# Regrouping one tile's TensorE work in the mixing stage: shared product with logits, turn inside the attention's projection

## The reference, cut to what matters

```python
x  = ln_affine(DN_ALPHA * x + gate1 * (concat(rms_norm(att), rms_norm(lru)) @ w_out), ln1_g, ln1_b)
u  = ln_plain(x) * (1 + scale2) + shift2
scores = sigmoid(u @ w_router)                     # 64 experts: the logits
# best 4 of 8 groups, best 6 experts of them, weights scaled to a sum of 2.5
g, up = split(u @ w_sh_in, 2)                      # the shared expert, 256 + 256 columns
shared = (silu(g) * up) @ w_sh_out
y = ln_affine(DN_ALPHA * x + gate2 * (routed + shared), ln2_g, ln2_b)
```

## Time and profile before

| | |
|---|---|
| median of 3 runs | 2910.28 us (2909.89 to 2911.74) |
| the profiled execution | 2911.56 us |
| its span, first to last instruction | 2909.7 us |
| mean granted TensorE clock | 0.978 of full speed |
| busy: TensorE, VectorE, ScalarE, GpSimd | 95%, 54%, 24%, 37% |
| mixing: first projection, experts' first product | 986.06 us, 1477.20 us |

### The profile page before, as it was taken

One profiled execution on the slowest core, in us unless ns is written; L12 is line 12 of the kernel. 1 busy time (PEld: TensorE's weight loads), 2 busy tenths in 40 slices (PEclk: granted clock), 3 DMA queues, 4 the chain that ended last, 5 costly groups with the idle time before them and its releaser, 6 DMA issues.

```text
span 2909.7 us, 31340 instructions
## 1 busy us (share of the span) xinstructions
PE 2750.7 (95%) x9145; PEld 1322.5 (45%) x9145; DVE 1584.6 (54%) x2551; ACT 692.2 (24%) x1204; POOL 1075.5 (37%) x1129
## 2 busy tenths in 40 slices
PE   6999999899999899899899999999999999999991
PEld 2345444455555454454444444444444444444440
DVE  3467356778877467787743333333333333344336
ACT  2354254366666211112100000000000000000004
POOL 2002000100000113233456665666665666565554
PEclk9999999999999999999999999999999999999996
DMA  8531010310000311221178798987888788899847
GB/s 336 192 114 55 17 34 8 129 42 12 12 12 8 142 44 66 87 80 59 59 247 252 202 322 246 294 257 188 271 232 251 184 247 247 258 304 292 237 94 253
DMA packets 188242, 464.37 MB, mean 160 GB/s; under 512 B 21500, under 2 KB 46270, under 8 KB 186750
## 3 DMA queue, kind: packets, MB, share of 16 engines
q1 hardware_dynamic: 137246, 311.89, 30.1%
q0 software_dynamic: 50912, 151.41, 21.3%
HBM read 359.28 MB, written 99.75 MB: 158 GB/s over the span
## 4 chain that ended last, share of the span: by engine, by line
PE 58%; DVE 5%; DMA 1%; issue 1%; POOL 1%; ACT 0%; DVEq 0%; POOLq 0%
PE mx_pH L1270 30%; PE mx_pU L1287 15%; PE mx_pA L1877 3%; PE mx_pH L1901 3%; PE mx_pL L1877 2%; PE mx_pU L1924 2%; PE mx_pB L1257 1%; DVE ring L1401 1%; DVE mx_st L1713 1%; DMA s_acc<-mx_wso,ex_sidx 1%; PE mx_pB L1913 1%; PE mx_pA L1901 0%; PE mx_pU L1887 0%; POOL mx_sm L1584 0%; DMA kT<-in_w_out 0%
## 5 line engine op out<-in xcount | busy, mean ns | idle before, releaser
L1270 PE MATMUL mx_pH<-ring,mx_wsi 128*128 (+1 forms) x2080 | 937.1, 593 | 5.0 <-DVE mx_wsi L1184 3.0
L1104 POOL DMA_INDIRECT kT<-s_u,ex_gidx x516 | 570.9, 1106 | 158.9 <-issue 153.2
L1270 PEld LDWEIGHTS mx_pH<-ring,mx_wsi 128*128 128x128 f32 x2080 | 385.5, 190 | 442.2 <-issue 442.2
L1287 PE MATMUL mx_pU<-qT,mx_hT 128*128 x1040 | 467.6, 592 | 1.5 <-DVE mx_wso L1211 1.5
L1184 DVE STREAM_TRANSPOSE mx_wsi<-kT 128x1024 f32<-128x1024 f32 x130 | 161.6, 1243 | 323.9 <-DMA kT<-s_u,ex_gidx 323.5
L1287 PEld LDWEIGHTS mx_pU<-qT,mx_hT 128*128 128x128 f32 x1040 | 197.5, 190 | 250.0 <-issue 250.0
L1128 POOL DMA_INDIRECT s_acc<-mx_wso,ex_sidx x130 | 212.2, 1633 | 188.6 <-DVE mx_wso L1211 126.5
L1211 DVE SCALAR_TENSOR_TENSOR mx_wso<-mx_pU,mx_wsi 128x1024 f32<-128x1024 f32 x130 | 166.9, 1284 | 194.9 <-PE mx_pU L1287 190.1
L1158 ACT ACTIVATE mx_hT<-mx_pB 128x256 f32<-128x256 f32 x130 | 49.9, 384 | 866.8 <-PE mx_pB L1257 866.8
L1188 DVE TENSOR_TENSOR mx_h<-mx_silu,mx_pH 128x256 f32<-128x256 f32 x130 | 54.6, 420 | 320.8 <-ACT mx_silu L1148 320.4
L638 PE MATMUL fr_pF<-fr_uT,fr_wf 128*128 128x512 f32 x512 | 224.9, 595 | 1.3 <-ACT fr_uT L332 1.0
(11 more groups left out here) (312 smaller groups left out, 3162.7 us busy)
## 6 DMA issues: line engine op xcount, KB each, us to landing
ring<-in_w_exp_in SPq DMA_DIRECT2D x64, 2048.0 KB, 12.8
qT<-in_w_exp_out SPq DMA_DIRECT2D x64, 1024.0 KB, 15.7
fr_wq<-in_w_ada SPq DMA_DIRECT2D x32, 512.0 KB, 4.8
kT<-s_u,ex_gidx POOLq DMA_INDIRECT x520
fr_wf<-in_w_in SPq DMA_DIRECT2D x16, 512.0 KB, 5.6
s_u<-v SPq DMA_DIRECT2D x16, 512.0 KB, 2.7
ring<-s_acc SPq DMA_DIRECT2D x16, 512.0 KB, 12.9
y<-ring SPq DMA_DIRECT2D x16, 512.0 KB, 3.7
```

What stands on the lines that cost most here:

```text
L1104: nc.gpsimd.indirect_dma_start(xg[:, u, g, :], None, u2_q, bass.IndirectOffsetOnAxis(ap=gidx[:, u, g:g + 1].bitcast(U32), axis=0)).then_in ...
L1270: m = nc.tensor.matmul(pH[:], xT[:, u, k, :], wi[:, bass.ds(slot, 1), k, :].rearrange("p a f -> p (a f)"), start=(k == 0), stop=(k == KD - 1))
L1287: m = nc.tensor.matmul(pY[:, h, :], hT[:, c, :], wo[:, bass.ds(slot, 1), c, h * 512:(h + 1) * 512].rearrange("p a d -> p (a d)"), start=(c ...
```

## The change

The logits of a tile become part of its shared product. The router's weights move into the tile of the shared weights, as columns 0 to 63 of each contraction slice. Up to tile LATE, `shared_in` is now two products: 64 + 256 = 320 columns (logits and the silu half) into `pH`, and 256 columns (the up half) into `pB`, which has a semaphore `up_mm`; the separate logits are left only behind LATE.

TensorE's order in iteration i (1 to LATE) becomes: att(i) half 0; turn(i); att(i) half 1; shared_in(i); lru(i+1) half 0; gated(i); rank(i-1); lru(i+1) half 1; shared_out(i). The lru product of a tile stands one iteration earlier.

On VectorE `gate(i-1)` moves from ahead of `add_att(i)` into the second statistics of `norms(i)`, between the statistics and the aggregate; `add_shared(i-1)` moves from `norms(i)` into `router(i-1)`, ahead of the one-hot of the six experts. On ScalarE `scores` comes before `gated_rows` and reads `pH`. On SP the store of a tile's sum comes one iteration later, and the load of x stands directly behind it.

```diff
...
   sem = lambda n: ctx.enter_context(nc.semaphore("mx_" + n))
-  wr, wsi, wso = sb("mx_wr", [P, KD, N_EXP]), sb("mx_wsi", [P, KD, 2 * D_E]), sb("mx_wso", [P, NB, D_E // P, D])
+  wsi, wso = sb("mx_wsi", [P, KD, 2 * D_E + N_EXP]), sb("mx_wso", [P, NB, D_E // P, D])
   rb, ln, iota, tokf = sb("mx_rb", [P, N_EXP]), sb("mx_ln", [P, 2, D]), sb("mx_iota", [P, N_EXP]), sb("mx_tokf", [P, 1])
...
   R1, R2, V1, V2 = range(4)
-  LOG, RNK = 0, 64
+  UP, LOG, RNK = 0, D_E, D_E + N_EXP
+  FIRST = N_EXP + D_E
...
       load_x(1)
-      sp.dma_start(wsi[:], w_sh_in.rearrange("(k p) f -> p k f", p=P)).then_inc(w_in, 16)
+      sp.dma_start(wsi[:, :, N_EXP:], w_sh_in.rearrange("(k p) f -> p k f", p=P)).then_inc(w_in, 16)
       gate2 = lambda b: mod_d[b:b + 1, 5 * D:6 * D].partition_broadcast(P)
...
       sp.dma_start(g2[:], gate2(0)).then_inc(g2_in, 16)
-      for dst, src in ((wr[:], w_router), (rb[:], router_bias.partition_broadcast(P)), (iota[:], iota_d.partition_broadcast(P))):
+      for dst, src in ((wsi[:, :, 0:N_EXP], w_router), (rb[:], router_bias.partition_broadcast(P)), (iota[:], iota_d.partition_broadcast(P))):
           sp.dma_start(dst, src).then_inc(r_in, 16)
...
                   load_wo(c)
-          if 0 < i <= LATE:
-              store_z(i - 1)
+          if 2 <= i <= LATE + 1:
+              store_z(i - 2)
+          if i >= 2 and i + 1 < NT:
+              load_x(i + 1)
           sp.wait_ge(u2_ready, i + 1)
...
               load_wo(7)
-          if i and i + 2 < NT:
-              load_x(i + 2)
           if i == KT:
...
           act.wait_ge(ut_mm, i)
-          if i > 1:
-              act.wait_ge(log_mm, i - 1)
+          if 1 < i <= LATE + 1:
+              act.wait_ge(up_mm, i - 1)
+          elif i > 1:
+              act.wait_ge(log_mm, i - 1 - LATE)
           if LATE < i < NT:
...
       def silu(i):
           act.wait_ge(h_mm, i)
...
               act.wait_ge(h_ready, i - 1)
-          nc.scalar.activation(silu_of(i), bank_of(i)[:, 0:D_E], ACT.Silu).then_inc(silu_ready, 1)
+          nc.scalar.activation(silu_of(i), bank_of(i)[:, N_EXP:FIRST] if i <= LATE else bank_of(i)[:, 0:D_E], ACT.Silu).then_inc(silu_ready, 1)
...
       def scores(i, logits):
-          act.wait_ge(log_mm, i)
+          if i <= LATE:
+              act.wait_ge(h_mm, i)
+              logits = pH[:, 0:N_EXP]
+          else:
+              act.wait_ge(log_mm, i - LATE)
           if i > 2:
...
               silu(i)
-              gated_rows(i)
           scores(i, pB[:, LOG:LOG + N_EXP])
+          if i <= LATE:
+              gated_rows(i)
       silu(LATE + 1)
...
-      def stats(z, which, eps, var_col, done):
+      def stats(z, which, eps, var_col, done, amid=None):
           for c in range(2):
...
           passed(dve, apart)
+          if amid is not None:
+              gate(amid)
           step(nc.vector.bn_aggr(mv[:, which, :], st[:].rearrange("p a s -> p (a s)")))
...
           dve.wait_ge(x1_ready, i + 1)
-          stats(z, 1, EPS, V2, var2)
+          stats(z, 1, EPS, V2, var2, i - 1 if 0 < i <= LATE else None)
           if i >= 2:
...
           step(nc.vector.scalar_tensor_tensor(u, z, mv[:, 1, 0:1], mrow[:, i // KT, 1, :], ALU.subtract, ALU.mult))
-          if 0 < i <= LATE:
-              add_shared(i - 1)
           dve.wait_ge(rstd2, i + 1)
...
           dve.wait_ge(silu_ready, i + 1)
-          nc.vector.tensor_tensor(gated_of(i + 1), silu_of(i + 1), bank_of(i + 1)[:, D_E:2 * D_E], ALU.mult).then_inc(h_ready, 1)
+          up = bank_of(i + 1)[:, D_E:2 * D_E]
+          if i < LATE:
+              dve.wait_ge(up_mm, i + 1)
+              up = pB[:, UP:UP + D_E]
+          nc.vector.tensor_tensor(gated_of(i + 1), silu_of(i + 1), up, ALU.mult).then_inc(h_ready, 1)
-      def router(i):
+      def router(i, amid=None):
           by_rank = lambda a, n: a.unsqueeze(1).to_broadcast([P, n, a.shape[1]])
...
           step(nc.vector.tensor_copy(gf[:, 1, :], gi[:, 1, :]))
+          if amid is not None:
+              add_shared(amid)
           step(nc.vector.tensor_tensor(oh[:], by_rank(iota[:], TOP_K), by_item(gf[:, 1, 0:TOP_K], N_EXP), ALU.is_equal))
...
                   fold(c)
-          if 0 < i <= LATE:
-              gate(i - 1)
           add_att(i)
...
           if i:
-              router(i - 1)
+              router(i - 1, i - 1 if i <= LATE else None)
       ranks(NT - 2)
...
+      def lru_half(i, h):
+          if i and h == 0:
+              pe.wait_ge(l_added, i)
+          if i == KT and h == 0:
+              pe.wait_ge(wo_folded, GQ)
+          m = project(pL, 1, lruT, i, h)
+          if h:
+              m.then_inc(pl_mm, 1)
       def project(out, which, src, i, h):
...
               pe.wait_ge(r_in, 48)
+          if i <= LATE:
+              for k in range(KD):
+                  m = nc.tensor.matmul(pH[:, 0:FIRST], uT(i, k), wsi[:, k, 0:FIRST], start=(k == 0), stop=(k == KD - 1))
+              m.then_inc(h_mm, 1)
+              if i > 1:
+                  pe.wait_ge(h_ready, i - 1)
+              if i > 2:
+                  pe.wait_ge(slots_ready, i - 2)
+              for k in range(KD):
+                  m = nc.tensor.matmul(pB[:, UP:UP + D_E], uT(i, k), wsi[:, k, FIRST:], start=(k == 0), stop=(k == KD - 1))
+              m.then_inc(up_mm, 1)
+              return
           for k in range(k0, k1):
-              m = nc.tensor.matmul(bank_of(i), uT(i, k), wsi[:, k, :], start=(k == 0), stop=(k == KD - 1))
+              m = nc.tensor.matmul(bank_of(i), uT(i, k), wsi[:, k, N_EXP:], start=(k == 0), stop=(k == KD - 1))
           if k1 == KD:
...
           pe.wait_ge(h_ready, i)
+          if i <= LATE:
+              pe.wait_ge(ez_ready, i)
           for c in range(FC):
...
           for k in range(KD):
-              m = nc.tensor.matmul(out, uT(i, k), wr[:, k, :], start=(k == 0), stop=(k == KD - 1))
+              m = nc.tensor.matmul(out, uT(i, k), wsi[:, k, 0:N_EXP], start=(k == 0), stop=(k == KD - 1))
           m.then_inc(log_mm, 1)
...
           pe.wait_ge(ez_ready, read)
+          pe.wait_ge(h_ready, min(read, LATE))
           if i > 1:
...
+      lru_half(0, 0)
+      lru_half(0, 1)
       for i in range(NT):
           if i:
-              pe.wait_ge(l_added, i)
-          if i == KT:
-              pe.wait_ge(wo_folded, GQ)
-          project(pL, 1, lruT, i, 0)
-          project(pL, 1, lruT, i, 1).then_inc(pl_mm, 1)
-          if i:
-              turn(i)
               pe.wait_ge(a_added, i)
...
           if i:
+              turn(i)
+          project(pA, 0, attT, i, 1).then_inc(pa_mm, 1)
+          if i:
               pe.wait_ge(ut_copied, i)
...
               shared_in(i)
-          project(pA, 0, attT, i, 1).then_inc(pa_mm, 1)
-          if 0 < i <= LATE:
+              lru_half(i + 1, 0)
               gated(i)
-          if i:
-              if i > 1:
-                  pe.wait_ge(ez_ready, i - 1)
-              if i > 2:
-                  pe.wait_ge(slots_ready, i - 2)
-              logits(i, pB[:, LOG:LOG + N_EXP])
-          if 0 < i <= LATE:
+              if i >= 2:
+                  rank(i - 1, i)
+              lru_half(i + 1, 1)
               shared_out(i)
-          if i >= 2:
+          elif i:
+              if i == LATE + 1:
+                  pe.wait_ge(h_ready, LATE)
+              pe.wait_ge(ez_ready, i - 1)
+              pe.wait_ge(slots_ready, i - 2)
+              logits(i, pB[:, LOG:LOG + N_EXP])
+          if i > LATE:
               rank(i - 1, i)
+          if (i == 0 or i > LATE) and i + 1 < NT:
+              lru_half(i + 1, 0)
+              lru_half(i + 1, 1)
```

More of the change, by code:

```diff
@@ L1486, in mixing @@
             [sem("u2_stored0"), sem("u2_stored1")])
-        ut_mm, ut_copied, h_mm, silu_ready, h_ready, ht_mm, ht_copied = (sem("ut_mm"), sem("ut_copied"), sem("h_mm"), sem("silu_ready"), sem("h_ready"),
+        up_mm, ut_mm, ut_copied, h_mm, silu_ready, h_ready, ht_mm, ht_copied = (sem("up_mm"), sem("ut_mm"), sem("ut_copied"), sem("h_mm"), sem("silu_ready"), sem("h_ready"),
                                                                         sem("ht_mm"), sem("ht_copied"))
@@ L1655, in _ @@
                     silu(i)
+                scores(i, pB[:, LOG:LOG + N_EXP])
+                if i <= LATE:
                     gated_rows(i)
-                scores(i, pB[:, LOG:LOG + N_EXP])
             silu(LATE + 1)
@@ L1958, in _ @@
                     shared_in(i)
-                project(pA, 0, attT, i, 1).then_inc(pa_mm, 1)
-                if 0 < i <= LATE:
+                    lru_half(i + 1, 0)
                     gated(i)
-                if i:
-                    if i > 1:
-                        pe.wait_ge(ez_ready, i - 1)
-                    if i > 2:
-                        pe.wait_ge(slots_ready, i - 2)
+                    if i >= 2:
+                        rank(i - 1, i)
+                    lru_half(i + 1, 1)
+                    shared_out(i)
+                elif i:
```

(8 more changed lines are left out.)

## The result

The changed kernel takes **2893.76 us** (median of four runs, 2891.93 to 2896.62), the kernel before 2910.86 beside it: a ratio of 0.994, 95% interval 0.9926 to 0.9954, so 17.1 us less. 2893.3 was predicted. The profiled execution took 2891.93 with a span of 2889.4, against 2911.56 and 2909.7 before.

What follows compares the result with a forecast made beforehand. TensorE's list was taken to bound most mixing tiles, VectorE the stage's end. Tiles of 26.46 us, a warm start and the earlier refold less turn 8's wait gave 17.0 us: 2894.6 profiled, 2893.3 median, range 2888 to 2903.

Steps and rivals of the forecast that it cites:

- What bounds: Mixing stage, tiles 1 to 6 and 8 to 12: TensorE's list sets the end, 27.36 us a tile before.
- The merged passes: Shared product with logits: passes of 320 and 256 columns take 7.74 us instead of 8.60, 0.86 off each tile.
- The tile: TensorE's new order in an ordinary tile of the mixing stage sums to 26.46 us, with no added hand-off cost.
- VectorE's round: VectorE's work per tile ends at 24.8 us, leaving 1.7 us slack; shared sum 1.8 us ahead of the turn.
- Start: Stage start: att 1's first half fills TensorE's 4.23 us gap, so turn 1 comes warm at 1012.61.
- Refold: Weight refold after tile 7: att 8 starts 15.5 us earlier, but turn 8 waits 3 to 5 us for shared sum 7.
- the slow price: After turn 8's idle, TensorE was taken to run slow: 1.69 us for the turn, 4.6 for the att half.
- Covered edits: ScalarE, SP and GpSimd edits and the router's weights load stay hidden; the load may land up to 7 us later.
- The sum: VectorE adds att 13 at 1349.4 instead of 1366.44, a gain of 17.0 us carried to the stage's end.
- A: Rival: merged passes pay weight load beside columns and cost the same, giving 2901.9 us; chance 0.04.
- C: Rival: turns wait for the shared sum in every tile, slower than before, 2919.7 us at 4.2 late; chance 0.05.
- B: Rival: only the merge pays, the reordering gives back its start and refold gains, 2901.7 us; chance 0.05.

Runs made afterwards that it cites:

- Experiment 4: Changed kernel without the merged product: shared product of 512 columns again, the logits' 16 passes of 64 right behind it; 2903.52 us, ratio 0.9968 to the kernel before.
- experiment 7: The changed kernel itself, unaltered, measured again beside other kernels; 2893.53 us, ratio 0.9935 to the kernel before.
- Experiment 8: Changed kernel with shared sum 7 alone moved right behind the refold's last fold, out of the router; 2890.88 us, ratio 0.9926 to the kernel before.
- Experiment 5: Changed kernel with the turn ahead of the first half of the attention's projection instead of between its halves; 2921.68 us, ratio 1.0035 to the kernel before.
- experiment 1: Kernel before with the merged 320- and 256-column products, old order kept except ScalarE's exponential ahead of its rows copy; 2916.01 us, ratio 1.0013.
- experiment 2: Merged product in the old order, as in experiment 1, with the ranks' product moved between gated rows and shared output; ratio 1.0014 to the kernel before.
- experiment 3: Experiment 1's kernel with the first normalisation's last pass cut to 64 of 1024 columns in tiles 1 to 12; tile 27.21 us, median not compared.

## Why the prediction was right, point by point

- **What bounds.** Right: TensorE's list in tiles 1 to 6 and 8 to 12, busy throughout at 1.00 but for the 0.46 us of tile 2 below.
- **The merged passes.** 320 columns were priced at 0.269 us and cost 4.31/16 = 0.269; 256 at 0.216 and cost 3.45/16 = 0.216. The product took 7.76 for 7.74. Experiment 4, which differs in this alone, has a tile 0.89 longer where 0.86 was the term. The Trainium skill ("TensorE: Matmul & The Clock Gate", Part 3, section "The mechanism") says that a weight load overlaps matmuls in flight only where it goes to another row group; read as in the prediction, by which load and columns add up and nothing is saved, this does not hold for these passes: the window of the tile above has 15.15 us of weight loads (PEld) inside 26.50 us, and a pass costs 0.84 ns per column at 256, 320 and 512. The same section also lets a load into the background weight buffer go ahead of matmuls in flight; no run here shows which buffer these loads went to.
- **The tile.** 26.46 predicted, 26.47 measured; hand-offs between accumulation groups cost 0.01.
- **VectorE's round.** Counted from VectorE adding att: shared sum at 19.14 of the round predicted, 18.9 measured; its lead on the turn 1.8, as measured; slack ahead of att 1.7 predicted, 1.96 measured. The gate waited 0.34 us where I had 0.14 (it came at 7.83 instead of 7.77), since the up half's result follows its slot by a latency, without effect.
- **Start.** Turn 1 was put 26.55 us into the stage, warm, and came at 26.50, warm. Tile 2's second fold was to cost 0.4; the tile took 26.93, 0.46 more than the others.
- **Refold.** Att 8 was to start at 216.3 and started at 216.0; turn 8 at 224.7, measured 224.2; att 8 was to be added at 231.0, measured 230.5. Att 7 was added 0.4 us later than forecast (196.07 for 195.6), and att 8 started 0.7 sooner behind it than forecast; the two misses offset each other, which is luck. The choice of the slow price (1.69 and 4.6, in all 6.3) was right in sum, 1.28 and 4.75 by the starts, and 0.99 and 5.03 in experiment 7. Experiment 8 shows that this wait was a real cost of the change. It took back 3.1 to 3.9 us of stage where I had expected 4.
- **Covered edits.** The store and load of x, the list writes and the exponential ahead of the rows nowhere show as a wait of TensorE in tiles 2 to 6. The first shared product did not wait for the router's weights: it started at 1015.17, right behind its att half.
- **The sum.** Att 13 was to be added 17.0 us earlier; it came 17.56 earlier in the stage, and the stage ended 17.23 earlier.

**The rivals.** A is out by the passes themselves. C did not occur. Experiment 5 shows its wait costing somewhat more than I gave it: 22.2 us of stage without the 5.1 at the start, where C's sum gives 11 x 1.74 = 19.1. B said that only the merge pays. It was the opposite, and this is where my working was weakest: it took 8.6 us as the merge's own worth, whatever the order. Experiments 1 and 4 make the four corners (stage against before's):

| | passes of 512 and 64 | passes of 320 and 256 |
|---|---|---|
| old order | 0 | +3.8 |
| new order | -6.6 | -17.2 and -16.4 |

Without the slow first passes of that execution the -6.6 is -8.1, and the merge is worth 8.3 to 9.1 us in the new order, near ten tiles of 0.89. The forecast didn't need the missing corner, since it added up TensorE's list in the new order directly. But a reader of it would have built the merge by itself for 8.6 us and lost 3. What the new order does for the merge is to put the products behind both att halves, out of the way from att to u to turn to att, and to give lru halves as cover for gate and copy. That the loop sets the tile in the old order is shown by experiments 2 and 3 together. The +3.8 splits into 0.9 up to att 1, 1.1 from there to att 6, 1.9 to att 8 and 0.7 to att 13, less 0.8 behind it; experiment 2 has 1.1, 2.1 and 0.7 for the three stretches in the middle. Of the 1.9, the longer product is 0.9 and an att half that ran slower, behind 6.31 us of idle instead of 3.58, is 0.4 (5.55 by the starts for 5.11); why the att half also started 0.6 later is open.

Left open: whether the 1.75 us by which front and attention ended earlier is spread. Their instructions are the same, and the eight kernels' mixing stages started between 983.83 and 985.74, all earlier than before's 986.06, of which only one execution has a trace.

## What to carry to other kernels

Work that an engine does between two dependent steps is cover as well as cost: before taking it out, list what ran behind it (here a copy, and the write of u), and sum the loop over the other engines as well as the engine's own list. The gain is at most the distance to the second longest of these, and work that is moved can lengthen one of them, as the logits did here. When a reordering makes a consumer wait for work on a busy engine, give it its place for the tiles where that engine has more to do (a fold, a reload), not only for the ordinary one: the ordinary tile of experiment 5 was foreseen to 0.1 us, and its stage missed by 8 (19 us over the changed kernel's expected, 27.4 measured).

## What the runs showed of the hardware

A narrow fp32 pass is held up by something other than its columns, a pass of 256 is not: 64 columns cost 1.73/16 = 0.108 us apiece, 256 cost 0.216, 320 cost 0.269, 512 cost 6.87/16 = 0.429. Per column of the last three that is 0.84 ns each time. The eight transposes of a turn, of 128 columns each, take 0.87 us, 0.109 apiece: as much as 64 columns of a product.

Idles of TensorE and the granted clock behind them: 0.80, 1.55 and 2.22 us left the work behind fast (turns 0.93 and 0.90, an att half 3.51 by the starts), 3.18, 3.70, 4.23 and 4.52 left it slow (the att half behind the last 4.91 instead of 3.60), and so did the 3.58 of the earlier trace rows (5.27). The idle of 3.56 in the earlier trace rows left a fast turn. In the tiles behind the twelfth shorter ones went either way: experiments 1 and 2 both idle 2.43 us ahead of turn 14, which took 1.09 us at a granted clock of 1.00 in the one (1380.60 to 1382.00), 1.97 at 0.50 in the other (1382.54 to 1384.50); in after, the recurrence's product behind 2.14 us of idle had 0.73 (1369.92 to 1375.50). So the length of the idle alone does not decide.

With the router's weights landing in 256-byte pieces, the queue that issues stood still behind their load; TensorE did not wait longer for them. SyncE's timeline of after:

```profile
992.25 1.14 SPq L1532 DMA_DIRECT2D mx_wsi<-in_w_router  x1
993.43 9.40 SPq L1532 DMA_DIRECT2D mx_rb<-in_router_bias  x1
1002.87 0.43 SPq L1532 DMA_DIRECT2D mx_iota<-in_iota  x1
```

The next load behind it took 9.40 us to issue (0.60 before), and 9.47 to 10.18 in the eight experiments, which have the same layout, and the loads after it went out 7 to 9 us later in the stage: iota at 1002.87 where the earlier trace rows have 995.87, 8.75 later from the stage's start. The page counts 1024 more packets under 512 bytes. The landing did not suffer: the router's weights landed 13.8 us after their issue (13.6 before), and iota, issued so much later, 4.6 us after its issue instead of 13.3, at 23.2 us of the stage as against 23.1. No wait of TensorE followed from it: turn 1 and the first shared product came when VectorE and the att half let them. The Trainium skill ("Perfetto Trace Analysis", section "What "DMA-bound" means") says that the window shown on an issuing queue is descriptor generation rather than movement; the rows agree in that the 9.40 us stand at the issue of a load of 32 KB, whose landing took 12.9 us from issue, hardly more than the 12.3 before. Nor can they be put down to that load's own descriptors: its layout is as before, when its issue took 0.60.
